# A two-layer hybrid diffusion step: scan keys merged into two buffers, first scan products moved to the projections, scan norm per tile, context units among the latent ones

## The reference, cut to what matters

```python
def trunk_layer(x, cond, lb, cached, ...):              # context: c_ctx, latent: c
    mod = jax.nn.silu(cond) @ mod_w + mod_b             # (6 * 1024): twelve rows of 512
    h = rms_norm(x, norm1_g) * (1.0 + sc1) + sh1
    qa, ia, fza, fzb, ga, qg, kg, vg, qw, kw, vw = split_proj(h @ w_in)
    o_a, s_a = hgrn_mixer(qa, ia, fza, fzb, ga, lb, a_norm_g, s0)
    o_g = blocked_attention(rope_2d(qg), concat(rope_2d(kg), ck_g), concat(vg, cv_g))
    o_w = banded_attention(rope_2d(qw), rope_2d(kw), vw, ck_w, cv_w, sink)
    x = x + g1 * (jnp.concatenate([o_a, o_g, o_w], axis=-1) @ w_out)
    x = x + g2 * moe(rms_norm(x, norm2_g) * (1.0 + sc2) + sh2, ...)

def hgrn_mixer(qa, ia, fza, fzb, ga, lb, norm_g, s0):
    q, v = jax.nn.silu(hd(qa)), hd(ia)
    # f = lb + (1 - lb) * sigmoid(z), k = (1 - lb) * sigmoid(-z), forward and backward
    # S_t = f_t * S_(t-1) + k_t v_t^T,   o_t = q_t S_t
    o = rms_norm(o_f + rev(o_b), norm_g) * jax.nn.sigmoid(hd(ga))
```

## Time and profile before

| | |
|---|---|
| median of 3 runs | 1650.66 us (1650.44 to 1658.09) |
| the profiled execution | 1649.77 us, span 1647.9 us |
| TensorE busy | 1391.0 us, 84% of the span |
| VectorE, ScalarE, GpSimd busy | 561.5, 357.7 and 207.2 us |
| mean granted clock of TensorE | 0.903 |
| HBM | 230.38 MB read, 34.41 MB written |

### The profile page before, as it was taken

The page is one execution under the profiler, slowest core; times in us unless marked ns, Lnnn a source line. Parts: engine busy times, 40 slices in busy tenths (PEclk is TensorE's granted clock), DMA queues, the critical chain, the costliest instruction groups (busy, mean ns, idle before and its releaser), DMA issues. The chain is left out here.

```text
span 1647.9 us, 18573 instructions
## 1 busy us (share of the span) xinstructions
PE 1391.0 (84%) x6686; PEld 873.6 (53%) x6687; DVE 561.5 (34%) x1202; ACT 357.7 (22%) x777; POOL 207.2 (13%) x187
## 2 busy tenths in 40 slices
PE   3999988898879959999659999789886993999990
PEld 1577645777745434444235774567785552444440
DVE  0204523555423321211161152456444334111116
ACT  3210012333411201111151000233342110111112
POOL 0001023221010000000110000432201000000003
PEclk9999986999979869999769999789998995999995
DMA  9600032417052559999442000533201223699945
GB/s 344 217 0 4 4 106 103 153 52 297 1 202 79 195 199 324 367 372 370 166 181 60 4 1 4 174 136 103 103 4 61 75 102 115 230 366 372 364 160 204
DMA packets 114442, 262.64 MB, mean 159 GB/s; under 512 B 10153, under 2 KB 18881, under 8 KB 114369
## 3 DMA queue, kind: packets, MB, share of 16 engines
q1 hardware_dynamic: 100688, 211.84, 36.1%
q0 software_dynamic: 8064, 29.36, 4.8%
q10 hardware_dynamic: 5616, 20.45, 3.1%
HBM read 230.38 MB, written 34.41 MB: 161 GB/s over the span
## 5 line engine op out<-in xcount | busy, mean ns | idle before, releaser
L1755 PE MATMUL PS<-W,T 128*128 128x512 f32 x544 | 245.3, 605 | 4.5 <-ACT T L1808 4.5
L1755 PEld LDWEIGHTS PS<-W,T 128*128 128x128 f32 x544 | 105.2, 194 | 137.6 <-issue 131.9
L1428 PE MATMUL PS<-W,T 128*128 128x512 f32 x320 | 144.5, 606 | 0.0
L617 PE MATMUL PS<-W,hT 128*128 128x384 f32 x320 | 129.8, 487 | 0.0
L1773 PE MATMUL PS<-W,T 128*128 128x512 f32 x272 | 127.2, 612 | 1.4 <-ACT T L1832 1.4
L980 PE MATMUL PS<-T 128*128 128x64 f32 x864 | 109.6, 279 | 3.2 <-ACT T L1101 1.9
L980 PEld LDWEIGHTS PS<-T 128*128 128x128 f32 x864 | 102.7, 194 | 15.4 <-issue 8.7
L1428 PEld LDWEIGHTS PS<-W,T 128*128 128x128 f32 x320 | 61.1, 196 | 70.5 <-issue 70.5
L584 PE MATMUL PS<-hT,W 128*128 128x512 f32 x192 | 98.3, 594 | 0.0
L1873 DVE TENSOR_TENSOR T<-PS,T 128x256 f32<-128x256 f32 x34 | 14.5, 426 | 243.9 <-ACT T L1819 243.9
L954 PE MATMUL PS<-T 64*128 64x128 f32 (+3 forms) x480 | 70.7, 411 | 16.6 <-ACT T L1101 11.6
(11 more groups left out here) (268 smaller groups left out, 1881.1 us busy)
## 6 DMA issues: line engine op xcount, KB each, us to landing
W<-in_w_gate_up SPq DMA_DIRECT2D x34, 2048.0 KB, 12.2
W<-in_mod_w SPq DMA_DIRECT2D x19, 2048.0 KB, 8.1
W<-in_w_down SPq DMA_DIRECT2D x34, 1024.0 KB, 10.6
y_rows<-T ACTq DMA_DIRECT2D x34, 512.0 KB, 8.6
W<-in_w_in SPq DMA_DIRECT2D x8, 2048.0 KB, 14.6
W<-in_w_out SPq DMA_DIRECT2D x2, 4096.0 KB, 13.8
T<-gate_lines SPq DMA_DIRECT2D x16, 512.0 KB, 7.2
y_rows<-cst SPq DMA_DIRECT2D x1, 7680.0 KB, 27.6
```

Source lines behind the costliest of these rows:

```text
L617: pe.matmul(out[:, 0:QW].rearrange("p (j v d) -> p j v d", v=KVH, j=G), lhsT, w[:, 0:QW].rearrange("p (v j d) -> p j v d", v=KVH, j=G), st ...
L1428: last = pe.matmul(PS[:, 4 + b, :], oT[:, t % 2, k, :], wout[:, k, half(b)], start=(k == 0), stop=(k == KC - 1))
L1755: last = pe.matmul(PS[:, 2 + par, :], hgT[:, par, k, :], w[:, k, :], start=(k == 0), stop=(k == KC - 1))
```

## The change

- The scan's first products (queries times gates, and the first widening) move from GpSimd's start of the attention block to the end of its projection block, behind the last query and key item. `Am` is no longer cleared; `Sv` is cleared after level 2, since the first widening's buffer now lies on it.
- `KM` becomes two buffers, used in turn by level. ScalarE merges the keys of level 1 at the start of the block and those of level n+1 before the fourth product of level n; GpSimd scales keys when the level's merge is done, while TensorE works on the level, and scales the queries after it.
- The units are ordered anew: latent pairs in order, a context pair after the first, third and fifth.
- The side steps get a quota per step: 5 in the first, 4 in a context step, 2 in a global and 3 in a window latent step. The modulation rows stand after levels 1 to 7, the last two behind level 7.
- The scan's norm is done per tile, the mean one step after the tile's output, the product two steps after; the gate is multiplied with the norm weight on GpSimd beforehand.
- SyncE puts two more weight loads ahead of the state loads, which wait for the later clearing.

```diff
-        KM = W[:, on0:on0 + 2 * TOK].rearrange("p (f n) -> p f n", f=2)
+        KM = [W[:, KC * INW - 2 * TOK:], W[:, on0:on0 + 2 * TOK]]
+        BP[2] = W[:, sv0:sv0 + 4 * TOK // 2].rearrange("p (d n) -> p d n", d=2)
...
+            def widen(pool, lv):
+                wider = BP[2 * LEVELS[lv - 1]]
+                for d in range(2):
+                    last = pool.tensor_tensor(wider[:, d, :], pairs(factors(lv), d)[:, :, 0], pairs(factors(lv), d)[:, :, 1],
+                                              ALU.mult)
+                return last
...
                 def _(pool):
...
+                    pool.wait_ge(s_z, QK_DONE)
+                    pool.wait_ge(s_qm, 2)
+                    for d in range(2):
+                        last = pool.tensor_tensor(qd[:, 1 - d, :], qq, fgate[:, d, :], ALU.mult)
+                    last.then_inc(s_hm, 1)
+                    flow(widen(pool, 1))
...
+            latent = [(t, j) for t in range(1, NT) for j in range(G)]
+            groups = []
+            for n, tj in enumerate(latent):
+                groups.append(tj)
+                if n % 2 == 0 and n // 2 < G:
+                    groups.append((0, n // 2))
...
+            mods = [[("mod_rows", n), ("mod_turn", n)] for n in range(MOD1, 12)]
             for lv in range(NLEV):
                 side_steps += [("level", lv, t) for t in range(NT)]
-                side_steps += [("mod_rows", MOD1 + lv), ("mod_turn", MOD1 + lv)]
+                if lv >= 1:
+                    side_steps += mods[lv - 1]
+            side_steps += mods[NLEV - 1] + [("gate_cols", 0)]
...
-            THIRDS = 3
+            quota = [(2, 2, 1)] + [(1, 1, 2) if units[u][0] == 0 else (1, 1, 0) if units[u][2] == 0 else (1, 1, 1)
+                                   for u in range(1, U)]
...
+            norm_mean = {t: out_step[t] + 1 for t in range(NT)}
+            norm_out = {t: out_step[t] + 2 for t in range(NT)}
...
-                    sp.wait_ge(s_hg, 2)
+                    for n in range(MOD1 + 2, MOD1 + 4):
+                        load_mod2(n)
+                    sp.wait_ge(s_hg, 1)
...
-                    pool.memset(Am, 0.0).then_inc(s_hg, 1)
-                    pool.memset(Sv, 0.0).then_inc(s_hg, 1)
...
                     for lv in range(1, NLEV):
+                        if lv >= 2:
+                            flow(widen(pool, lv))
+                        pool.wait_ge(s_km, lv)
+                        if lv == 1:
+                            pool.wait_ge(s_side, side_at["level", 0, NT - 1] + 1)
+                        scale_keys(pool, lv)
                         pool.wait_ge(s_side, side_at["level", lv, NT - 1] + 1)
+                        scale_queries(pool, lv)
+                        if lv == 2:
...
+                            pool.memset(Sv, 0.0).then_inc(s_hg, 1)
+                    pool.tensor_tensor(ga.rearrange("p t (a d) -> p (t a) d", d=HD), ga.rearrange("p t (a d) -> p (t a) d", d=HD),
+                                       ang[:, :].unsqueeze(1).to_broadcast([P, NT * AH, HD]), ALU.mult)
+                    for t in range(NT):
+                        pool.wait_ge(s_hp, t + 1)
+                        pool.tensor_tensor(small[:, 88 + AH * t:92 + AH * t], small[:, 112 + AH * t:116 + AH * t],
+                                           minus_half[:, 0:AH], ALU.pow).then_inc(s_hq, 1)
...
+                        if lv >= 3:
+                            act.wait_ge(s_side, side_at["level", lv - 2, NT - 1] + 1)
+                        act.activation(KM[lv % 2].rearrange("p (m r j) -> p m r j", r=2, j=h),
...
-                        if kind == "mod_turn":
-                            lv = at[0] - MOD1 + 1
-                            if lv < NLEV:
-                                merge_keys(lv)
+                        if kind == "level" and 1 <= at[0] < NLEV - 1 and at[1] == NT - 2:
+                            merge_keys(at[0] + 1)
...
+                    merge_keys(1)
                     for step in range(U + 2):
...
+                    def mean(t):
+                        out = small[:, 112 + AH * t:112 + AH * t + AH]
+                        dve.wait_ge(s_hx, t + 1)
+                        flow(dve.tensor_reduce(out, osq[:, t, :].rearrange("p (a d) -> p a d", d=HD), AX.X, ALU.add))
+                        dve.tensor_scalar(out, out, 1.0 / HD, EPS, ALU.mult, ALU.add).then_inc(s_hp, 1)
+
+                    def normed(t):
+                        dve.wait_ge(s_hq, t + 1)
+                        flow(dve.tensor_tensor(osum[:, t, :], osum[:, t, :], ga[:, t, :], ALU.mult))
...
-                    dve.wait_ge(s_hx, NT)
-                    flow(dve.tensor_reduce(ms, osq.rearrange("p t (a d) -> p (t a) d", d=HD), AX.X, ALU.add))
...
-                    dve.wait_ge(s_hq, 1)
-                    dve.wait_ge(s_gst, 16)
```

More of the change, by code:

```diff
@@ L669, in _ @@
                                            ALU.pow).then_inc(s_rp, 1)
+                    qq = QQ.rearrange("p f n -> p (f n)")
+                    flow = chain(pool, s_hf)
+                    pool.wait_ge(s_z, QK_DONE)
+                    pool.wait_ge(s_qm, 2)
+                    for d in range(2):
+                        last = pool.tensor_tensor(qd[:, 1 - d, :], qq, fgate[:, d, :], ALU.mult)
+                    last.then_inc(s_hm, 1)
+                    flow(widen(pool, 1))
                 @block.vector
@@ new lines, in program @@
+            groups = []
[3 more added lines that the diff above has]
+                    groups.append((0, n // 2))
+            units = []
+            for t, j in groups:
+                for wnd in range(2):
+                    if t == 0:
+                        keys, moff = [0], None
+                    elif not wnd:
+                        keys, moff = list(range(1, NT + 1)), None
+                    else:
+                        keys = ([t - 1] if t > 1 else []) + [t, NT] + ([t + 1] if t < NL else [])
+                        moff = 0 if t > 1 else P
+                    units.append((t, j, wnd, keys, moff))
@@ L808, in turned_bufs @@
             def turned_bufs(u):
[L810 to L813, removed]
+                return prT[units[u][2]]
             def vector_part(u):
@@ L835, in program @@
             NSIDE = len(side_steps)
-            SIDE_START = 0
-            THIRDS = 3
+            quota = [(2, 2, 1)] + [(1, 1, 2) if units[u][0] == 0 else (1, 1, 0) if units[u][2] == 0 else (1, 1, 1)
+                                   for u in range(1, U)]
+            quota = [q for step in quota for q in step] + [0] * 6
+            sides_done = [0] + [sum(quota[:n + 1]) for n in range(len(quota))]
+            assert sides_done[-1] >= NSIDE
             side_at = {step: i for i, step in enumerate(side_steps)}
@@ L847, in sides_before @@
             def sides_before(step, part):
-                return min(NSIDE, max(0, THIRDS * (step - SIDE_START) + part))
+                return min(NSIDE, sides_done[3 * step + part])
+            out_step = [next(step for step in range(U + 2) if sides_before(step + 1, 0) > side_at["out", t])
+                        for t in range(NT)]
+            norm_mean = {t: out_step[t] + 1 for t in range(NT)}
+            norm_out = {t: out_step[t] + 2 for t in range(NT)}
+            assert max(norm_out.values()) <= U + 1
             with nc.Block() as block:
```

124 lines of the change are left out of this document (52 added, 72 removed).

## The result

The changed kernel took 1679.4 us in the median of four runs (1671.8 to 1686.3), the kernel before 1652.2 beside it: a ratio of 1.0172, 95% interval 1.0131 to 1.0214. It is 1.7% slower, where 1601 had been forecast. The profiled execution is the slowest of the four (1686.25 us, span 1684.4); the others' times fall as their mean granted clock rises from 0.888 to 0.900.

A forecast was written before the change was run, and what follows sets the result against it. TensorE was taken as the limit, so time off the attention-and-scan block comes off the end: 18.0+15.1 for the blocks, 2x7 for the norm, 2x1.5 for the next block's clock, 50.1 us in all, giving 1601, range 1570 to 1638.

The forecast's parts named there:

- Order and quota: Attention-and-scan block: same 78 side steps in new order and pace; block length 212.5 us against 230.5 and 227.6.
- waits from new neighbours: Attention-and-scan block: 4.5 us in step 0, 8 in context steps, 3 for modulation turns; together 15.5.
- the start's clock: Block's first two steps: at 1.2 GHz products cost some 8 us more; the middle, 4, was taken.
- context steps stay slow: Rival, context steps: product-and-evacuation chain at 1.2 GHz again, 16 us, only the end gained; near 1634, chance 0.20.
- Norm per tile: End of block: next product 7.97 us earlier, 1 us of 0 to 7 charged; net 7 per layer.
- The next block's clock: Start of the block after attention: a shorter gap may keep 2.4 GHz; 1.5 us of 0 to 4.3 per layer.
- GpSimd's moved products: End of projections: two 5.73 us products and a 2.9 us widening run beside TensorE; costed at nothing, at most 8.6 per layer.
- two key buffers: Scan levels: ScalarE's merge no longer waits for the last level's readers; removes 5.5 us of TensorE waits.
- The rival of a stalled merge: Rival, ScalarE: merges wait for GpSimd's scaled keys and queue other work; at 6 us each some 1672, chance 0.06.
- GpSimd holding VectorE: Rival, last steps: GpSimd's five reciprocal roots hold VectorE, 4.6 us per layer; 1610, chance 0.06.

The follow-up runs named there:

- The fastest run: Changed kernel with context units first, three side products a step for 18 steps, then two, and unread turns in the first eight steps: 1575.9 us, ratio 0.9544.
- the two runs with half of the quota: Changed kernel with three side products in context steps, not four: 1639.2 us, 0.9920; or three in global latent steps, not two: 1652.7 us, 0.9981.
- the version with its products in the block: Changed kernel with context units first, even pace, GpSimd's first products and widening back at the attention block's start: 1622.1 us, ratio 0.9819.

## Why the prediction was wrong, step by step

- **Order and quota: the step that failed.** It priced the waits from new neighbours at 15.5 us a layer and the start's clock at 4, and everything else at 2.4 GHz. The block took 251.8 and 260.0 us, not 212.5, and TensorE ran at a mean of 0.85 and 0.81 instead of near 1. The fastest run shows how the 39.3 and 47.5 us divide: it keeps TensorE busy 182.4 us, 9.5 of them unread, so the same 1561 instructions take about 173 us at 2.4 GHz. By that estimate the forecast held 177 us of work and 35.5 of waits; measured were 206.1 and 45.7 in layer 0, 216.3 and 43.7 in layer 1. So about 29 and 39 us of the error are the clock, 10 and 8 are waits. The working priced side products by their duration in latent pairs with three a step, where they fill pauses; the quota took one out of each global latent step, which opened a pause of 0.7 us in the mean before the next scores, and put it into context steps behind another through the same banks. Undoing the quota gives 58 to 62 us.
- **The clock.** The prediction looked for it in the first two steps only. The rival "context steps stay slow" named the cause, but gave it 16 us a layer, in the context steps alone; the pauses of the latent steps and the end of the block cost clock too.
- **Norm per tile: mis-sized by the whole of its bound.** I charged 1 us of 0 to 7 a layer, with the sentence that a late maximum has room. On the kernel before it cost 7.2 and 9.5 and gave 8.2: nothing. It is not that every piece lay on the path. Several tiles' pieces fell in one step and held up one maximum, and behind the pause of 2.3 to 2.8 us the block ran at 1.2 GHz to its end. That is not so each time: in layer 1 of the run with the context first and the even pace a pause of 2.82 us was followed by 12 us at 2.4 GHz before the clock fell. With one tile to a step the profiled blocks show it nearly free, as charged: 248.2+237.9=486.1 us, against 243.1+241.6=484.7 with the norm at the end. The medians don't bear this out in full: with both gaps 8.2 us shorter the run is 10.6 us faster, and by the ratios (1.0097 against 1.0115) only 3, within the noise.
- **The next block's clock** (1.5 of 0 to 4.3): lost. The output projection's first turns take 1.94 us, as before. The slow end of the block is not the whole reason: with the quota and the norm spread both blocks end at 1.00, with the same gap, and these turns take 1.94 us there too. They took 1.06 only in three of the four blocks of the two runs with half of the quota; why there is open.
- **GpSimd's moved products, two key buffers: right.** The products run ahead of the block, for 8.7 us as estimated, and cost nothing that shows; the merge is gone from TensorE's waits. In GpSimd's timeline of the changed kernel:

```profile
195.57 5.91 POOL L721 TENSOR_TENSOR W<-T 128x1280 f32<-128x1280 f32 x2 [3.00 <-PE PS L666]
201.45 2.82 POOL L575 TENSOR_TENSOR W<-T 128x640 f32<-128x640 f32 x2
```
  The rival of a stalled merge didn't come; the kernel got slower in another way.
- **GpSimd holding VectorE.** Not at the norm's roots, but at the key scalings: VectorE's two-column operation that takes 0.16 us when alone (L1227 at 248.14) took 1.49 at 265.18, within GpSimd's scaling of 263.57 to 266.66; TensorE's next level product waited 1.94 us for VectorE, until 267.36, and 1.2 us of that fall in this operation. It agrees with the rule of the Trainium skill (SBUF — State Buffer, Who interferes with whom) that the prediction cites.

```profile
263.57 3.09 POOL L585 TENSOR_TENSOR T<-T,W 128x640 f32<-128x640 f32 x2
265.18 1.49 DVE L1227 TENSOR_TENSOR small<-small,sink 128x2 f32<-128x2 f32 x1
267.36 1.23 PE L1049 MATMUL PS<-W 64*128 64x128 f32 x8 [1.94 <-DVE hT L1266]
```

- **What was right in sum.** Even pace and spread norm in the changed order take 1602.9 us, about the forecast 1601. That the sum fits there is luck in part and no proof of its terms: its 212.5 us for a block is near the 213.2 and 215.0 of that run, but there the waits are 29.5 and 29.0 us, less than the 35.5 in the forecast, and the clock costs about 11 and 13 instead of 4.

What stays open: how the 33 us between the kernel before with the norm per tile and the version with its products in the block divide between the second key buffer, the later modulation rows, the clearings and the order of loads; and whether the number or the place of the norm's pieces does the harm. No run separates them.

## What to carry to other kernels

Price an order of work not only by the durations of what it moves but by the pause that it leaves where the work stood: here one product less between a turn and the next scores, and one more behind a product through the same banks, cost 58 us in a kernel of 1650. When work is cut into pieces, look at how many pieces fall into one step, and at what stands behind the engine that does them: several tiles' norm pieces in one step undid a gain of 16 us. And read the granted clock by stretches: a pause can be paid twice, once as a wait and again in the work after it.

## What the runs showed of the hardware

Work that nobody reads can pay. Sixty unread turns in the first eight steps of a block went with a clock of 1.00 in its first 60 us, for 0.74 and 0.69 without them, and the kernel became 0.8% faster, although they only add work. All six executions had a mean clock of 0.934 to 0.936, the five without them 0.916 to 0.922.

And the clock at a block's start is not fixed by its program: two runs with the same first 18 steps (context first, three sides a step) had 0.91 and 0.74 there in layer 0, and a third with the same steps had 0.91 in layer 0 and 0.74 in layer 1. The first two, with the norm spread and with the sides to step 29, and then the last with unread turns:

```profile
233.93:293.93 60.00, 48.27 (x429) 34.80 (x429) 33.29 (x71) 21.04 (x56) 26.09 (x21) 0.91 0.51 174
230.34:290.34 60.00, 50.38 (x376) 35.52 (x377) 30.79 (x64) 19.98 (x55) 25.16 (x21) 0.74 0.42 144
232.43:292.43 60.00, 55.37 (x520) 41.84 (x522) 35.08 (x79) 22.70 (x62) 26.15 (x21) 1.00 0.51 178
```

For 13 us the first two run alike, with the same waits to a few hundredths of a us; then the same four instructions take 0.66 us in the one and 1.11 in the other. What tipped it, no run shows.

```profile
247.15 0.66 PE L1019 MATMUL PS<-T 128*128 128x64 f32 x4
243.57 1.11 PE L1019 MATMUL PS<-T 128*128 128x64 f32 x4
```
